# One reciprocal for three of the four softmax sums of an attention step, in both attentions of a three-layer block

## The reference, cut to what matters

```python
def window_attention(q, k, v, k_ctx, v_ctx, sink):      # 16 heads in 4 groups, head size 64
    for n in range(8):                                   # blocks of 128 queries
        # keys: 256 of the context and the 384 around the block (256 at either end)
        p = softmax([sink, q @ k_ctx, where(|qpos - kpos| <= 128, q @ k, -1e30)])[1:]
        out[n] = p @ [v_ctx, v]

def fox_attention(q, k, v, log_f):                       # 8 heads, head size 64
    cum = cumsum(log_f)
    for i in range(8):                                   # blocks of 128 queries, causal
        p = softmax(where(kpos <= qpos, q @ k / 8 + cum[q] - cum[k], -inf))
        out[i] = p @ v
```

## Time and profile before

| what | value |
|---|---|
| runs shown | 2529.60, 2535.28, 2533.84 us, median 2533.84 |
| profiled execution | 2526.92 us, of which the span from the first to the last instruction is 2525.1 |
| PE busy | 2321.6 us, 92% of the span |
| DVE busy | 1425.4 us, 56% |
| POOL busy | 1375.9 us, 54% |
| ACT busy | 774.8 us, 31% |
| mean granted TensorE clock | 0.959 of 2.4 GHz |
| `attc`: first and last reciprocal | 823.3 and 1072.9 us from the start |
| `attf`: first and last reciprocal | 1475.0 and 1624.9 us from the start |

### The profile page before, as it was taken

How to read it: one execution, slowest core, us unless ns; L and a number is a source line. 1 busy time by engine, 2 the same in 40 slices (tenths; PEclk the granted TensorE clock), 3 DMA queues, 4 the chain that set the end, 5 groups by cost and what they waited for, 6 DMA issues and landing times. The chain is left out here.

```text
span 2525.1 us, 32202 instructions
## 1 busy us (share of the span) xinstructions
PE 2321.6 (92%) x11283; PEld 1915.7 (76%) x11283; DVE 1425.4 (56%) x2162; ACT 774.8 (31%) x1405; POOL 1375.9 (54%) x1372
## 2 busy tenths in 40 slices
PE   6898998999999999989879967899999999999995
PEld 2687888788887877878747756777788878888874
DVE  1754646567772899958989867738612212222236
ACT  3321112123221888823423247623310000000012
POOL 2536554842533788447779556656764733333360
PEclk9899999899999899989989979989999999999997
DMA  7436335513355665253143657552222311111121
GB/s 276 149 97 193 105 111 169 183 47 117 117 173 161 175 168 157 78 192 94 41 135 117 181 152 229 172 204 88 90 86 67 100 41 48 47 50 51 51 67 67
DMA packets 180302, 305.92 MB, mean 121 GB/s; under 512 B 34924, under 2 KB 73512, under 8 KB 178864
## 3 DMA queue, kind: packets, MB, share of 16 engines
q1 hardware_dynamic: 138336, 218.55, 29.5%
q10 hardware_dynamic: 41808, 85.31, 9.1%
HBM read 247.14 MB, written 56.66 MB: 120 GB/s over the span
## 5 line engine op out<-in xcount | busy, mean ns | idle before, releaser
L1009 POOL TENSOR_SCALAR WH<-RAW 128x512 fp32r<-128x512 f32 (+1 forms) x466 | 337.9, 725 | 900.6 <-PE PS L1129 747.6
L1127 PE MATMUL PS<-HXH,WH 128*128 128x512 f32 (+1 forms) x1904 | 757.3, 398 | 54.3 <-DVE HXL L2479 11.4
L1128 PE MATMUL PS<-HXL,WH 128*128 128x512 f32 (+1 forms) x1904 | 749.9, 394 | 0.0
L1129 PE MATMUL PS<-HXH,WL 128*128 128x512 f32 (+1 forms) x1904 | 749.2, 393 | 0.0
L1012 POOL TENSOR_TENSOR WL<-RAW,WH 128x512 fp32r<-128x512 f32 (+1 forms) x466 | 636.1, 1365 | 38.9
L1127 PEld LDWEIGHTS PS<-HXH,WH 128*128 128x128 f32 (+1 forms) x1904 | 360.7, 189 | 140.5 <-issue 13.4
L1129 PEld LDWEIGHTS PS<-HXH,WL 128*128 128x128 f32 (+1 forms) x1904 | 360.5, 189 | 79.5 <-issue 2.1
L1128 PEld LDWEIGHTS PS<-HXL,WH 128*128 128x128 f32 (+1 forms) x1904 | 360.8, 189 | 78.9 <-issue 3.9
L2384 DVE TENSOR_TENSOR TM<-PS,TM 128x512 f32<-128x512 f32 x44 | 28.4, 686 | 379.7 <-ACT TM L1810 379.7
L1810 ACT ACTIVATE TM<-PS 128x512 f32<-128x512 f32 x44 | 23.9, 596 | 556.1 <-PE PS L1129 556.1
L2397 DVE TENSOR_TENSOR Y<-PS,Y 128x2048 f32<-128x2048 f32 x40 | 91.7, 2292 | 120.9 <-PE PS L1129 120.7
(11 more groups left out here) (311 smaller groups left out, 4103.1 us busy)
## 6 DMA issues: line engine op xcount, KB each, us to landing
RAW<-in_ada_w SPq DMA_DIRECT2D x160, 256.0 KB, 2.9
RAW<-in_w_ffn_in SPq DMA_DIRECT2D x224, 128.0 KB, 2.1
RAW<-in_w_in_ab SPq DMA_DIRECT2D x88, 256.0 KB, 2.7
RAW<-in_w_in SPq DMA_DIRECT2D x56, 256.0 KB, 2.6
RAW<-in_w_ffn_out SPq DMA_DIRECT2D x56, 256.0 KB, 2.6
XR<-XX ACTq DMA_DIRECT2D x3, 4096.0 KB, 12.1
XX<-XR ACTq DMA_DIRECT2D x3, 4096.0 KB, 12.6
RAW<-in_w_in_c SPq DMA_DIRECT2D x40, 256.0 KB, 2.6
```

The costliest lines, as they stand in the source:

```text
L1009: g.tensor_scalar(WH[:, sw, 0:m], RAW[:, r, 0:m], 1.0, 0.0, ALU.mult, ALU.add).then_inc(gpsimd_done, 1)
L1127: mm(out, wh, xh, start=first, stop=False, **kw)
L1128: mm(out, wh, xl, start=False, stop=False, **kw)
L1129: return mm(out, wl, xh, start=False, stop=last, **kw)
```

## The change

In both attentions DVE no longer takes a reciprocal for every head. For heads 0 and 1 it does nothing. In the place where it took that of head 2 it takes one reciprocal of columns 0 to 2 (128x3), and then, as before, that of head 3 (128x1). Its waits stay those of head 2 and head 3. The marks that POOL waits for follow: the multiplications of heads 0, 1 and 2 now wait for the same instruction. POOL's own code, with the order of its multiplications and modulation tiles, is unchanged, and so is that of all other engines.

```diff
-                        if 1 <= u <= 128:
+                        if 1 <= u <= 128 and (u - 1) % 4 >= 2:
 
                             y, b, hh = u - 1, (u - 1) // 4 % 2, (u - 1) % 4
+                            h0 = 0 if hh == 2 else 3
                             dve.wait_ge(scalar_done, upto("exp", "c", y))
                             if y >= 8:
                                 dve.wait_ge(gpsimd_done, upto("P", "c", y // 4 - 2, hh))
-                            v.reciprocal(RC[b][:, hh:hh + 1], SU[b][:, hh:hh + 1]).then_inc(vector_done, 1)
-                            did(vector_done, ("rc", "c", y))
+                            v.reciprocal(RC[b][:, h0:hh + 1], SU[b][:, h0:hh + 1]).then_inc(vector_done, 1)
+                            did(vector_done, *[("rc", "c", y - hh + x) for x in range(h0, hh + 1)])
...
-                        if 1 <= u <= 64:
+                        if 1 <= u <= 64 and (u - 1) % 4 >= 2:
```

More of the change, by code:

```diff
@@ L2657, in _ @@
                                 dve.wait_ge(gpsimd_done, upto("P", "f", y // 4 - 2, hh))
-                            v.reciprocal(RC[b][:, hh:hh + 1], SU[b][:, hh:hh + 1]).then_inc(vector_done, 1)
-                            did(vector_done, ("rc", "f", y))
+                            v.reciprocal(RC[b][:, h0:hh + 1], SU[b][:, h0:hh + 1]).then_inc(vector_done, 1)
+                            did(vector_done, *[("rc", "f", y - hh + x) for x in range(h0, hh + 1)])
                         z = step_at(u, OTA_AT["f"], 16)
```

## The result

The changed kernel takes 2603.71 us (median of 4 runs, 2597.92 to 2606.76), the kernel before 2532.83 us on the same chip (4 runs). The ratio is 1.0277, with a 95% interval from 1.0257 to 1.0298: 71 us slower, where 79 were forecast and 2613 us predicted. In the profiled execution the span went from 2525.1 to 2599.2 us, 74.1 more.

A forecast was written before the change was run, and what follows sets the result against it. The windowed attention, with PE, DVE and POOL all nearly full, would be bound by a loop through POOL's multiplications. 51.2 + 0.5 + 4 + 18 + 5 = 79 us on 2533.8 gives 2613 us, range 2571 to 2652.

The forecast's parts named there:

- Step length: Windowed attention: inner steps with a full modulation tile go from about 7.6 to 10.46 us through a closed loop.
- Its two halves: Windowed loop: joint reciprocal to POOL's end of head 3, 5.67 us; from there to the next reciprocal, 4.79 us.
- The sum without the clock: Windowed attention: 51.2 us from longer steps, 0.5 behind step 31 and 4 for the gate multiplication.
- The gate multiplication: Windowed attention: POOL's addition beside DVE's gate multiplication takes 2.14 instead of 1.30 us, about five steps, 4 us.
- The clock: Windowed attention: PE's stalls lower its clock, losing 1.7 us in about half of 21 steps, 18 us; bounds 0 and 54.
- the rival of a clock that stays up: Windowed attention: same loop without the 18 us for the clock, 2595 us; chance 0.20.
- The rival of a clock that stays low: Windowed attention: clock stays low throughout, 115 us lost, 2649 us; chance 0.12.
- The bound of 54: Windowed attention: upper bound of the clock loss, 27 steps x 2.0 us, the way back at 1.2 GHz.
- The forgetting attention: Forgetting attention: delayed multiplications, partly covered by POOL's waits for loads, lose 5 us; bounds -3 and +9.
- DVE's saving: Both attentions: fewer reciprocals save DVE 5.1 and 2.6 us, 7.7 together, a ceiling reached only if DVE sets the pace.
- DVE sets the pace: Attentions: POOL's delay is hidden and the kernel gains up to 7.7 us, 2526 us; chance 0.05.
- a looser loop: Windowed attention: next step starts during POOL's wait, only POOL's excess occupancy counts, 10 to 45 us, about 2560; chance 0.08.

The follow-up runs named there:

- With PE kept busy: Full change plus eight 128x512 products on PE before the first transposes of steps 2 to 24 of the windowed attention; 1.0255 of the kernel before.
- the later transposes: Full change with each tile of windowed transposes one part later: 1.0164; also both modulation tiles behind head 3: 1.0158; kernel before with that transpose move: 1.0139.
- a delay of one part: Joint reciprocal of heads 0 and 1 only, heads 2 and 3 with their own, in both attentions; 1.0013 of the kernel before.

## Why the prediction was right

*Step length.* It put inner steps at 10.46 us; they are 10.43 and 10.44 where the clock holds. Its two halves were 5.67 and 4.79; they are 5.64 and 4.79. Steps without a tile were put at 8.21 and are 8.19 to 8.21 (26 to 28). The six end steps (7, 8, 15, 16, 23, 24) were put at 9.2; with PE kept busy they are 9.1 to 9.6 between joint reciprocals, and in the changed kernel 9.0 to 9.4 and, for two of them behind a fall of the clock, 10.5.

*The sum without the clock.* 51.2, 0.5 and 4 make 55.7. With PE kept busy, the stretch from the first custom instruction of the attention to the last is 305.57 us against 250.43 before: 55.1. The terms for the attention were right to a us, the gate's by luck, as the next lines say.

*The gate multiplication* was put at 0.8 in five steps. It is 1.03 in three of them, 5, 13 and 21; in steps 9 and 17 the three multiplications were all but through. What is stretched is not POOL's addition, from which the 0.8 was taken, but its three multiplications (3.39 in place of 2.36):

```profile
878.28 3.39 POOL L1104 TENSOR_SCALAR PB<-PB,RC 128x640 f32<-128x640 f32 x3
```

The sum was near, the count and the instruction were not.

*The clock* was the term that was mis-sized: 18 us forecast, 11.9 measured. It fell in 9 of the 24 steps with tiles in the profiled run, at 1.3 to 1.6 us each, not in half of them at 1.7. By the total the rival of a clock that stays up, 2595, came as near to the measured 2603.7 (8.7 us off) as the forecast of 2613 (9.3 off); what tells them apart is the granted clock, which fell, and the 11.9 us. The rival of a clock that stays low is out, since the clock was back at 1.00 within a step each time. That the stalls would bring the low clock back in each step, as that rival has it, came true in 9 of 24. The bound of 54 for this term counted 27 steps where the prediction's own list has 24 with a tile, and the 37 us at the low end of the range is nowhere worked out.

*The forgetting attention* was put at 5 with bounds of -3 and 9; it is 7 alone (4 to 9 by the interval), and 4.3 us in the profile of the full change. With the measured sizes the terms are 55.1, 11.9 and 7, together 74, and the profiled execution is 74.1 longer.

*DVE's saving.* The 7.7 us were called a ceiling, to be had if DVE sets the pace. It doesn't, in steps with tiles or without, and nothing of them entered the sum, because the loop covers them. The rival "DVE sets the pace" falls with that, and so does that of a looser loop: the way back was 4.79 us to the hundredth. That DVE would set steps without a tile stood only in the expectation of the later transposes.

*What the profile would show* came as stated, but for one bound: PE's matmuls wait 47.6 us for POOL, where 50 or more were named. DVE's busy share from 823 to 1142 us is 230.0 of 319, 0.72, where about 0.75 was named.

## What to carry to other kernels

Before several small instructions are joined, ask who waits for the first of them and what that engine does next in its own order: here 0.16 us of VectorE's time in each step was bought with 3 us of GpSimd work that moved from a gap into the path. If an engine waits for the result of a loop that it feeds itself, write the loop out and add it up; it counts only where it is longer than the step it replaces, which is why a delay of one part cost 0.1% and of two parts 2.8%. A busy share of 98% does not say that an engine sets the pace: VectorE had it in the steps without tiles, and two instructions fewer left them as long as they were. Nor does a closed chain that adds up to the step: any chain that repeats does that. It binds only if each engine in it really waits for the one before.

## What the runs showed of the hardware that was not expected

In a stall PE does only three single transposes in about three microseconds (in step 3 at 856.57, 858.26 and 859.03). Its clock fell to 1.2 GHz behind some of these stalls and not behind others, 9 of 24 in one execution; behind that of step 3 it stayed at 2.4 GHz. The run with the same code for the windowed attention, and the forgetting one as before, had its long steps in other places: step 3 at 10.4 in both, step 2 at 10.42 in place of 11.83, step 10 at 11.99 in place of 10.45. What decides between them no run shows. Work without any use, put into the stall, kept the clock at 1.00. The next instruction on VectorE started 0.08 us behind a reciprocal of one column, and 0.09 us behind one of three (854.11 above, and the subtraction at 854.20).
